# A gated decoder layer on one NeuronCore: another split of the contraction in the gate stage, and two vector operations placed later

## The chip, the cores and the metric

One core of a Trainium2 chip runs the whole layer in one launch. The time is device microseconds (us), the median of three runs. TensorE (PE) multiplies, VectorE (DVE) and ScalarE (ACT) work beside it, SyncE (SP) issues most transfers from HBM and GpSimd (POOL) issues the rest. PE's granted clock was 0.999 of full speed.

## The reference, cut to what matters

```python
mod = jax.nn.silu(c) @ w_ada[l] + b_ada[l]                  # (2048) @ (2048, 6 * 2048)
sh1, sc1, gt1, sh2, sc2, gt2 = split(mod, 6)
h = rmsnorm(x, g_pre_mix[l]) * (1.0 + sc1) + sh1            # x: 256 tokens x 2048
proj = h @ w_in[l]            # GLA q/k/v/gate, a rank-16 factor, MoBA q/k/v, gate_a, gate_b
y_a = o_gla @ w_gla_out;  y_b = o_moba @ w_moba_out
merged = sigmoid(gate_a) * y_a + sigmoid(gate_b) * y_b
x = x + gt1 * rmsnorm(merged @ w_o, g_post_mix)
h = rmsnorm(x, g_pre_ffn) * (1.0 + sc2) + sh2
x = x + gt2 * rmsnorm(conv_ffn(h), g_post_ffn)              # up, conv of width 3, GELU gate, down
```

All is float32. A product is made of three passes: operands are split into a rounded part `hi` and a remainder `lo`, and hi*hi, hi*lo and lo*hi are summed in PSUM.

## The kernel before, in words

The contraction over 2048 channels runs over 16 k-tiles of 128. The kernel's first 232 us are the gate stage: columns `gate_a` and `gate_b` of `w_in` (4096 columns, eight blocks of 512). The trouble there is that `h` needs `sh1` and `sc1` first, which are themselves a product with 33.5 MB of `w_ada`. So the stage is cut along the contraction into five chunks, listed in `CHUNK`, and `K0` holds where each begins. For a chunk of n k-tiles the 16 pieces of `w_ada` that give its shift and scale are read first, each 128 x 2 x 128n elements. The text calls them units. DVE adds a unit times a column of silu(c) to `acc0` (`head_unit`, L978 and L981), PE turns the sum, DVE reduces it to `mods` (`shift_and_scale`, L1009 to L1014), ACT and DVE scale x to `h` and split it (`h_part`, `h_scale`, `h_lo`). This is called the turn to a chunk. Then PE works the chunk's eight slots, one for each block of 512 columns: a slot of n k-tiles is 6n matmuls of 512 columns (4n with `hi` weights, then 2n with `lo`). ACT rounds each slot's weights `raw` to `hi` (L561), DVE subtracts to get `lo` (L971). Partial sums are copied out of PSUM and back in between chunks (L640, L647), and the last chunk's are added by DVE (`gate_out`, L1110). Two slots for values lie in chunks 1 and 2, and one for the rank-16 columns (`W_LOW`) ahead of chunk 4.

What sets the order. SP issues in the order written: 16 units of chunk 0, then slot w's weights and two units of the next chunk (three at slots 5 and 6, none at slot 7), and so on, all on one queue. There are four `raw` buffers, so slot w's weights wait until PE has finished slot w-4 (`used`), and eight buffers for units, so a unit waits until DVE has used the one eight before it. DVE's order is written out too: in `for w in range(W_HEAD)` it takes some units (two, and four at the fifth slot of a chunk), then `split_lo(w + 3)`. At the fifth slot of chunk 2 it takes all of the first four units of chunk 4 before the `lo` of slot 7 of chunk 2, and the turn to chunk 3 follows that `lo`.

The first slot has only one chunk's worth of data to wait for and is worked in two halves (`first_slot`, `first_mods`): k-tiles 0 and 1, then the rest.

The other 67.1 MB of `w_ada` are 96 modulation units of 128 x 1024 elements, issued by POOL and added by DVE into `acc_a` or `acc_b` (`ada_unit`, L1000). Tables say how many DVE takes after each step: `UNITS_3` for the last nine slots of the gate stage, `UNITS_E`, `UNITS_H` and `UNITS_L` for the four heads, `UNITS_M` for the 16 steps of the merge. After the gate stage the first head step waits for the gate sum of slot 6 of chunk 4 (`gate_add`). In the merge DVE multiplies each block of 512 columns by its gates and adds (`merged`, L1287 to L1290), and PE transposes the result one step later (`merged_T`, L1848). The first steps of the output projection wait for all 96 modulation units.

Of the kernel before, what the change touches and what calls it, by code (L numbers as in the profile page):

```python
# [12 lines left out]
P = 128  # L13
# [3 lines left out]
def layer_kernel(nc, x, c, w_ada, b_ada, g_pre_mix, w_in, w_alpha_up, b_alpha, g_gla_head, w_gla_out,  # L17
# [28 lines left out]
    UP_ITERS = FFN // 256  # L46
    CHUNK = (3, 3, 3, 3, 4)
    NQ = len(CHUNK)
# [83 lines left out]

    UNITS_3 = {W_LOW + j: n for j, n in enumerate((0, 1, 1, 1, 2, 2, 2, 2, 1))}
    UNITS_H = [2, 1, 1, 1, 1, 1, 1, 2, 2, 2, 2, 2]
    UNITS_E = [2, 1, 1, 1, 1, 1, 0, 2, 2, 2, 2, 1]
    UNITS_L = [2, 1, 1, 1, 1, 1, 1, 2, 2, 1, 1, 1]
    UNITS_M = [0, 2, 2, 1, 1, 2, 0, 2, 1, 2, 1, 2, 1, 1, 0, 1]
    assert sum(UNITS_3.values()) + EARLY * sum(UNITS_E) + (HEADS - 1 - EARLY) * sum(UNITS_H) + sum(UNITS_L) + sum(UNITS_M) == 6 * KT

# [20 lines left out]
    with ctx:  # L160
# [207 lines left out]
        def _(sp):  # L368
# [41 lines left out]
            for w in range(W_HEAD):  # L410
                if w >= 4:
                    sp.wait_ge(used, w - 3)
                if w == 0:
                    c0 = C_GA + 512 * GATE_CB[0][0]
                    sp.dma_start(grid(0, 512)[:, 0:2, :], win[:, 0:2, c0:c0 + 512]).then_inc(half_in, 16)
                    for j in range(2):
                        cs = slice(256 * j, 256 * (j + 1))
                        fill(0, grid(0, 512)[:, 2:CHUNK[0], cs], win[:, 2:CHUNK[0], c0 + 256 * j:c0 + 256 * (j + 1)])
                elif w == W_LOW:
                    load_grid(w, win, 0, KT, C_LOW, P)  # L420
                elif GATE_SLOTS[w][0] == VALUE:
# [128 lines left out]
        def _(act):  # L550
# [72 lines left out]
            for k in range(2, CHUNK[0]):  # L623
                ins = act.activation(h32[:, k, :], xT[:, k, TOK:], ACT.Identity, bias=mods[:, M_SH1, k:k + 1], scale=mods[:, M_SC1, k:k + 1])
            link(ins)
            act.activation(hT[:, 2:CHUNK[0], 0:TOK], h32[:, 2:CHUNK[0], :], ACT.Copy).then_inc(first_hi, 1)
            act.wait_ge(arr[0], fills(0))
            act.activation(hi[:, 0, 1024:slot_elements(0)], raw[:, 0, 1024:slot_elements(0)], ACT.Copy).then_inc(hi_done, 1)
            split_hi(1)
# [320 lines left out]
        def _(dve):  # L950
# [91 lines left out]
            for half, done in ((0, unit_half), (1, unit_done)):  # L1042
                part = slice(256, P * CHUNK[0]) if half else slice(0, 256)
                a = acc0[:, 0, :, part]
                unit = unit_view(KT - 1)[:, :, part]
                dve.scalar_tensor_tensor(a, unit, scol[:, KT - 1:KT], a, ALU.mult, ALU.add).then_inc(done, 1)
            dve.wait_ge(cols_read, 3)

            def first_mods(half, done):
                qs = slice(2, CHUNK[0]) if half else slice(0, 2)  # L1050
                dve.wait_ge(done, 1)
# [7 lines left out]
            dve.wait_ge(xt_read, 1)  # L1059
            for k in (0, 1):  # L1060
# [479 lines left out]
        def _(pe):  # L1540
# [469 lines left out]
```

## Time and profile before

| | us |
|---|---|
| median of 3 runs | 1452.08 (1452.02 to 1455.47) |
| profiled execution, its own time | 1453.58 |
| its span, first to last instruction | 1451.8 |
| PE busy | 1420.3 (98%) |
| DVE busy | 1090.1 (75%) |
| ACT busy | 757.6 (52%) |
| chain that ended last | PE 88%, DMA 5%, DVE 4%, ACT 2% |

The span is the time from the first to the last instruction, and what lies around it is 1.8 us. PE is busy nearly all the time, so the time can change only where PE is idle, or if PE's own work changes. A transfer's landing is read from the row of the first instruction that waited for it: its start, where the idle time before it was ended by that DMA. A row with xN stands for N instructions in a row.

### The profile page before, as it was taken

The numbers are of one execution on the slowest core, as the hardware profiler recorded it, in microseconds if no ns is written. First come the engines' busy times: TensorE is split into PE (matmuls) and PEld (weight loads), VectorE is DVE, ScalarE is ACT, GpSimd is POOL, SyncE is SP. The second block draws the span as 40 slices with busy tenths as digits, with TensorE's granted clock in tenths as the row PEclk, the third lists the DMA queues.
The fourth block names the chain that finished last, engine by engine and source line by source line (L and its number), as shares of the span: only waits on it lengthen the run. The fifth ranks groups of instructions, "written<-read, shape, count | busy, mean of one in ns | idle before, by whom it ended". The sixth has DMA issues, their size and how long they took to land.

```text
span 1451.8 us, 19848 instructions
## 1 busy us (share of the span) xinstructions
PE 1420.3 (98%) x7298; PEld 1210.2 (83%) x7298; DVE 1090.1 (75%) x1163; ACT 757.6 (52%) x869; POOL 84.2 (6%) x165
## 2 busy tenths in 40 slices
PE   4999999999999999999999999999999999999998
PEld 3788778888888888878888888888888888888886
DVE  5999879988989888844887777787777666544545
ACT  6566663555545466334855445454455455344343
POOL 2000001111111111000000000000000000000000
PEclk9999999999999999999999999999999999999999
DMA  9999979988988878857486767676766565655553
GB/s 352 380 374 380 364 244 347 289 294 293 327 272 285 274 269 283 283 177 286 147 272 234 244 219 243 203 241 222 240 223 200 175 195 184 201 193 185 200 193 125
DMA packets 240570, 367.08 MB, mean 253 GB/s; under 512 B 12015, under 2 KB 178673, under 8 KB 239746
## 3 DMA queue, kind: packets, MB, share of 16 engines
q1 hardware_dynamic: 220576, 294.69, 61.1%
q0 software_dynamic: 18848, 69.23, 13.2%
q10 hardware_dynamic: 1090, 2.40, 0.4%
q8 instruction: 36, 0.59, 0.2%
q14 instruction: 20, 0.16, 0.0%
HBM read 364.18 MB, written 2.10 MB: 252 GB/s over the span
## 4 chain that ended last, share of the span: by engine, by line
PE 88%; DMA 5%; DVE 4%; ACT 2%; issue 1%; SPq 0%; DVEq 0%; ACTq 0%
PE ps L1542 87%; DMA raw<-in_w_in 2%; DVE acc L981 1%; DMA adar<-in_w_ada 1%; DMA ada<-in_w_ada 1%; ACT hi L561 1%; DMA raw<-in_w_gla_out 1%; DMA raw<-in_w_moba_out 0%; DVE lo L971 0%; DVE acc_a L1000 0%; DVE yt L1362 0%; PE ps L1848 0%; DVE x L1365 0%; SPq L405 0%; PE ps L1827 0%
## 5 line engine op out<-in xcount | busy, mean ns | idle before, releaser
L1542 PE MATMUL ps<-hT,hi 128*128 128x512 f32 x1936 | 465.8, 393 | 1.7 <-DVE GA L1110 0.9
L1542 PEld LDWEIGHTS ps<-hT,hi 128*128 128x128 f32 x1936 | 356.1, 188 | 72.7 <-DVE GA L1110 1.3
L561 ACT ACTIVATE hi<-raw 128x2048 fp32r<-128x2048 f32 (+1 forms) x123 | 222.3, 1808 | 238.1 <-DMA raw<-in_w_in 154.2
L971 DVE TENSOR_TENSOR lo<-raw,hi 128x2048 fp32r<-128x2048 f32 (+1 forms) x123 | 264.7, 2153 | 77.1 <-ACT hi L561 76.7
L1542 PEld LDWEIGHTS ps<-hT,lo 128*128 128x128 f32 x1920 | 246.1, 191 | 9.8 <-DVE lo L971 0.5
L1542 PE MATMUL ps<-hT,lo 128*128 128x256 f32 x1920 | 249.2, 283 | 0.1
L1490 DVE TENSOR_TENSOR lo<-raw,hi 128x2048 fp32r<-128x2048 f32 x88 | 199.0, 2290 | 32.5 <-ACT hi L914 32.3
L1542 PE MATMUL ps<-hi,hT 128*128 128x512 f32 x768 | 186.7, 393 | 2.2 <-ACT hi L561 1.9
L1542 PE MATMUL ps<-hi,asp 128*128 128x512 f32 x704 | 175.9, 389 | 0.0
L1542 PEld LDWEIGHTS ps<-hi,hT 128*128 128x128 f32 x768 | 142.1, 188 | 35.0 <-issue 4.5
L914 ACT ACTIVATE hi<-raw 128x2048 fp32r<-128x2048 f32 x88 | 165.9, 1906 | 8.8 <-DMA raw<-in_w_up 7.5
L1542 PEld LDWEIGHTS ps<-hi,asp 128*128 128x128 f32 x704 | 132.1, 188 | 27.4
L1521 DVE TENSOR_TENSOR lo<-raw,hi 128x2048 fp32r<-128x2048 f32 x40 | 91.7, 2292 | 49.7 <-ACT hi L936 49.7
L546 POOL DMA_DIRECT2D ada<-in_w_ada x128 | 67.7, 530 | 676.2 <-DVE acc_a L1459 294.7
L1542 PE MATMUL ps<-lo,hT 128*128 128x512 f32 x384 | 96.6, 390 | 0.4 <-DVE lo L971 0.2
L1542 PE MATMUL ps<-lo,asp 128*128 128x512 f32 x352 | 96.1, 389 | 0.0
L892 ACT ACTIVATE cv<-ps 128x512 f32<-128x512 f32 x44 | 26.4, 600 | 133.6 <-PE ps L1542 133.6
L981 DVE SCALAR_TENSOR_TENSOR acc<-adar,scol,acc 128x768 f32<-128x768 f32 (+1 forms) x73 | 78.1, 1071 | 12.4 <-DMA adar<-in_w_ada 8.7
L1542 PEld LDWEIGHTS ps<-lo,hT 128*128 128x128 f32 x384 | 71.9, 188 | 16.1 <-DVE lo L971 0.7
L903 ACT ACTIVATE asp<-aT 128x256 fp32r (+1 forms) x44 | 18.0, 416 | 124.5 <-PE ps L1542 124.5
L896 ACT ACTIVATE cv<-up,cols 128x256 f32<-128x256 f32 x88 | 48.2, 595 | 56.7 <-DVE up L1472 56.7
L1542 PEld LDWEIGHTS ps<-lo,asp 128*128 128x128 f32 x352 | 66.0, 188 | 14.0 <-DVE lo L971 0.4
(265 smaller groups left out, 1312.2 us busy)
## 6 DMA issues: line engine op xcount, KB each, us to landing
raw<-in_w_up SPq DMA_DIRECT2D x176, 512.0 KB, 4.4
raw<-in_w_in SPq DMA_DIRECT2D x146, 512.0 KB, 6.1
ada<-in_w_ada POOLq DMA_DIRECT2D x128, 512.0 KB, 5.4
raw<-in_w_down SPq DMA_DIRECT2D x88, 512.0 KB, 4.2
adar<-in_w_ada SPq DMA_DIRECT2D x64, 384.0 KB, 8.9
raw<-in_w_o SPq DMA_DIRECT2D x32, 512.0 KB, 4.7
adar<-in_w_ada SPq DMA_DIRECT2D x16, 512.0 KB, 9.9
raw<-in_w_gla_out SPq DMA_DIRECT2D x16, 512.0 KB, 4.9
```

The lines of the kernel that those rows point to most:

```text
L546: pool.dma_start(unit_buffer(u), wada[:, t, PART_COL[part]:PART_COL[part] + 1024]).then_inc(ada_in[unit_slot(u)], 16)
L561: act.activation(hi[:, w % 4, 0:n], raw[:, w % 4, 0:n], ACT.Copy).then_inc(hi_done, 1)
L892: act.activation(cv[:, :, :], ps[:, 2 * g:2 * g + 2, TOK:], ACT.Copy).then_inc(cross5, 1)
L896: act.activation(cv[:, ct, :], up[:, ct, 2:], ACT.Identity, scale=cols[:, ds(f + COL_CONV + 4 * FT, 1)], bias=cols[:, ds(f + COL_CB, 1)]). ...
L903: act.activation(asp[:, k, 0:TOK], aT[:, ds(kt, 1), :], ACT.Copy).then_inc(a_hi, 1)
L914: act.activation(hi[:, w % 4, :], raw[:, w % 4, :], ACT.Copy).then_inc(hi_done, 1)
L971: dve.tensor_tensor(lo[:, w % 4, 0:n], raw[:, w % 4, 0:n], hi[:, w % 4, 0:n].bitcast(F32), ALU.subtract).then_inc(lo_done, 1)
L981: ins = dve.scalar_tensor_tensor(a, unit_view(u), scol[:, t:t + 1], a, ALU.mult, ALU.add)
L1490: dve.tensor_tensor(lo[:, k, :], raw[:, k, :], hi[:, k, :].bitcast(F32), ALU.subtract).then_inc(lo_done, 1)
L1521: dve.tensor_tensor(lo[:, k, :], raw[:, k, :], hi[:, k, :].bitcast(F32), ALU.subtract).then_inc(lo_done, 1)
L1542: return pe.matmul(out_, lhsT, rhs, start=start, stop=stop, skip_group_check=open_sum)
```

## The change

`CHUNK` becomes 2, 3, 3, 4, 4. The first slot has two k-tiles now and is worked as k-tile 0, then k-tile 1 (`FIRST = 1`). One modulation unit leaves the table of the gate stage (slot 5 of chunk 4), one leaves step 10 of the merge, and one each is added at steps 13 and 15. The number of matmuls, of units and of bytes stays as it was.

```diff
-    CHUNK = (3, 3, 3, 3, 4)
+    CHUNK = (2, 3, 3, 4, 4)
+    FIRST = 1
...
-    UNITS_3 = {W_LOW + j: n for j, n in enumerate((0, 1, 1, 1, 2, 2, 2, 2, 1))}
+    UNITS_3 = {W_LOW + j: n for j, n in enumerate((0, 1, 1, 1, 2, 2, 1, 2, 1))}
...
-    UNITS_M = [0, 2, 2, 1, 1, 2, 0, 2, 1, 2, 1, 2, 1, 1, 0, 1]
+    UNITS_M = [0, 2, 2, 1, 1, 2, 0, 2, 1, 2, 0, 2, 1, 2, 0, 2]
...
-                    sp.dma_start(grid(0, 512)[:, 0:2, :], win[:, 0:2, c0:c0 + 512]).then_inc(half_in, 16)
+                    sp.dma_start(grid(0, 512)[:, 0:FIRST, :], win[:, 0:FIRST, c0:c0 + 512]).then_inc(half_in, 16)
...
-            act.activation(hi[:, 0, 0:1024], raw[:, 0, 0:1024], ACT.Copy).then_inc(half_hi, 1)
+            act.activation(hi[:, 0, 0:512 * FIRST], raw[:, 0, 0:512 * FIRST], ACT.Copy).then_inc(half_hi, 1)
...
-                part = slice(256, P * CHUNK[0]) if half else slice(0, 256)
+                part = slice(P * FIRST, P * CHUNK[0]) if half else slice(0, P * FIRST)
...
-                    ks = range(2, CHUNK[0]) if half else range(2)
+                    ks = range(FIRST, CHUNK[0]) if half else range(FIRST)
```

On SP's queue at the start of the program, before (`adar` are units, `raw` weights; the last number of a unit is 128n):

```order
L405 DMA adar<-in_w_ada 128x2x384 x16
L415 DMA raw<-in_w_in 128x2x512
L370 DMA raw<-in_w_in 128x256 x2
L405 DMA adar<-in_w_ada 128x2x384 x2
L370 DMA raw<-in_w_in 128x512
L370 DMA raw<-in_w_in 128x2x512
```

and now:

```order
L406 DMA adar<-in_w_ada 128x2x256 x16
L416 DMA raw<-in_w_in 128x512
L371 DMA raw<-in_w_in 128x256 x2
L406 DMA adar<-in_w_ada 128x2x384 x2
L371 DMA raw<-in_w_in 128x512 x2
```

The first 16 units are a third smaller, and so are the first slots' weights, while the units between them, which are chunk 1's, keep their size.

On DVE around the turn to chunk 3, before (`acc_90` takes units; the reduce and the two rows behind it make the shift and scale):

```order
L971 TENSOR_TENSOR lo<-raw,hi 128x1536
L978 TENSOR_SCALAR acc_90<-adar,scol 128x1024
L981 SCALAR_TENSOR_TENSOR acc_90<-adar,scol,acc_90 128x1024 x3
L971 TENSOR_TENSOR lo<-raw,hi 128x1536
L1009 TENSOR_REDUCE mods<-ps 128x2x3
L1012 TENSOR_TENSOR mods<-mods,cols 128x2x3
L1014 SCALAR_TENSOR_TENSOR mods<-mods,cols 128x3
```

and now:

```order
L972 TENSOR_TENSOR lo<-raw,hi 128x1536
L979 TENSOR_SCALAR acc_90<-adar,scol 128x1024
L982 SCALAR_TENSOR_TENSOR acc_90<-adar,scol,acc_90 128x1024 x3
L972 TENSOR_TENSOR lo<-raw,hi 128x1536
L1010 TENSOR_REDUCE mods<-ps 128x2x4
L1013 TENSOR_TENSOR mods<-mods,cols 128x2x4
L1015 SCALAR_TENSOR_TENSOR mods<-mods,cols 128x4
```

The order is the same: four units of chunk 4, a `lo`, the reduce. The reduce covers four k-tiles now.

On DVE between the gate sums of slots 5 and 6 of chunk 4, before:

```order
L1110 TENSOR_TENSOR GA<-GA,ps 128x2x512
L971 TENSOR_TENSOR lo<-raw,hi 128x2048
L1000 SCALAR_TENSOR_TENSOR acc_a<-ada,scol,acc_a 128x1024
L1000 SCALAR_TENSOR_TENSOR acc_a<-ada_114,scol,acc_a 128x1024
L1110 TENSOR_TENSOR GA<-GA,ps 128x2x512
```

and now:

```order
L1111 TENSOR_TENSOR GA<-GA,ps 128x2x512
L972 TENSOR_TENSOR lo<-raw,hi 128x2048
L1001 SCALAR_TENSOR_TENSOR acc_a<-ada,scol,acc_a 128x1024
L1111 TENSOR_TENSOR GA<-GA,ps 128x2x512
L972 TENSOR_TENSOR lo<-raw,hi 128x2048
```

One unit of two is gone. In the merge the single unit ahead of `merged` for block 2 (L1287) is gone in the same way.

## Rows read from the trace of the kernel before

**Rows 1.** Busy time of each engine, clock, DMA share and GB/s, by stretch.
```profile
core 0: us, PE busy (x) PEld busy (x) DVE busy (x) ACT busy (x) POOL busy (x), PEclk, DMA share, GB/s
20.00:140.00 120.00, 116.56 (x525) 94.24 (x524) 107.89 (x107) 77.16 (x83) 0.00 (x0) 1.00 1.06 377
140.00:160.00 20.00, 20.00 (x93) 16.58 (x92) 19.42 (x18) 11.98 (x13) 0.00 (x0) 1.00 1.05 386
176.00:232.00 56.00, 55.42 (x249) 44.70 (x247) 43.91 (x39) 30.96 (x25) 6.98 (x14) 1.00 0.86 280
```
**Rows 2.** PE's waits over the span: total us, times, longest.
```profile
PE ps L1542 <- ACT hi L561: 1.9, 4, 0.9
PE ps L1848 <- DVE GA L1290: 1.0, 2, 0.7
```
**Rows 3.** PE's timeline: start, duration, [idle before it, ended by].
```profile
30.02 1.16 PE L1542 MATMUL ps<-hi,hT 128*128 128x512 f32 x4
35.18 3.06 PE L1542 MATMUL ps<-hi,hT 128*128 128x512 f32 x12 [0.38 <-ACT hi L561]
...
145.48 1.52 PE L1542 MATMUL ps<-hi,hT 128*128 128x512 f32 x6
...
171.02 2.99 PE L1542 MATMUL ps<-hi,hT 128*128 128x512 f32 x12 [0.38 <-ACT hi L561]
...
202.26 3.79 PE L1542 MATMUL ps<-hi,hT 128*128 128x512 f32 x16
...
207.70 3.79 PE L1542 MATMUL ps<-hi,hT 128*128 128x512 f32 x16
...
225.82 3.79 PE L1542 MATMUL ps<-hi,hT 128*128 128x512 f32 x16
```
**Rows 4.** PE's timeline, first step of the heads.
```profile
232.28 3.94 PE L1542 MATMUL ps<-hT,hi 128*128 128x512 f32 x16 [0.86 <-DVE GA L1110]
```
**Rows 5.** ACT's timeline, the last transposed x and the first weights.
```profile
26.12 0.43 ACT L596 ACTIVATE xT<-ps 128x256 f32<-128x256 f32 x1
28.00 1.06 ACT L616 ACTIVATE hi<-raw 128x1024 fp32r<-128x1024 f32 x1 [1.45 <-DMA raw<-in_w_in]
```
**Rows 6.** ACT's timeline, rounding of slots' weights as they land.
```profile
75.67 1.50 ACT L561 ACTIVATE hi<-raw 128x1536 fp32r<-128x1536 f32 x1 [0.63 <-DMA raw<-in_w_in]
...
80.79 1.92 ACT L561 ACTIVATE hi<-raw 128x2048 fp32r<-128x2048 f32 x1 [2.71 <-DMA raw<-in_w_in]
...
169.39 1.49 ACT L561 ACTIVATE hi<-raw 128x1536 fp32r<-128x1536 f32 x1 [1.28 <-DMA raw<-in_w_in]
```
**Rows 7.** DVE's timeline at the turn to chunk 3.
```profile
137.23 2.67 DVE L981 SCALAR_TENSOR_TENSOR acc<-adar,scol,acc 128x1024 f32<-128x1024 f32 x2 [0.75 <-DMA adar<-in_w_ada]
139.82 1.75 DVE L971 TENSOR_TENSOR lo<-raw,hi 128x1536 fp32r<-128x1536 f32 x1
141.56 0.96 DVE L1009 TENSOR_REDUCE mods<-ps 128x6 f32<-128x768 f32 x1
```
**Rows 8.** ACT's timeline at the same turn.
```profile
143.00 1.10 ACT L607 ACTIVATE h<-xT,mods 128x256 f32<-128x256 f32 x2 [0.90 <-DVE mods L1014]
144.13 0.63 ACT L611 ACTIVATE hT<-h 128x512 fp32r<-128x512 f32 x1
```
**Rows 9.** DVE's timeline ahead of the gate sum of slot 6.
```profile
228.42 2.67 DVE L1000 SCALAR_TENSOR_TENSOR acc_a<-ada,scol,acc_a 128x1024 f32<-128x1024 f32 x2
231.01 1.21 DVE L1110 TENSOR_TENSOR GA<-GA,ps 128x1024 f32<-128x1024 f32 x1
```
**Rows 10.** DVE's timeline in the merge, ahead of the transposes of block 2.
```profile
589.47 1.28 DVE L1000 SCALAR_TENSOR_TENSOR acc_b<-ada,scol,acc_b 128x1024 f32<-128x1024 f32 x1
```
**Rows 11.** PE's timeline, the transposes of block 2.
```profile
594.32 1.09 PE L1848 MATMUL ps<-ident,GA 128*128 128x128 f32 x8 [0.67 <-DVE GA L1290]
```
**Rows 12.** DVE's timeline at the end of the merge.
```profile
608.83 2.29 DVE L971 TENSOR_TENSOR lo<-raw,hi 128x2048 fp32r<-128x2048 f32 x1 [1.78 <-ACT hi L561]
...
621.00 0.69 DVE L1296 TENSOR_TENSOR mT<-ps,mT 128x512 fp32r<-128x512 f32 x1 [2.18 <-ACT mT L770]
```

More of the change, by code:

```diff
@@ L414, in _ @@
                     c0 = C_GA + 512 * GATE_CB[0][0]
-                    sp.dma_start(grid(0, 512)[:, 0:2, :], win[:, 0:2, c0:c0 + 512]).then_inc(half_in, 16)
+                    sp.dma_start(grid(0, 512)[:, 0:FIRST, :], win[:, 0:FIRST, c0:c0 + 512]).then_inc(half_in, 16)
                     for j in range(2):
                         cs = slice(256 * j, 256 * (j + 1))
-                        fill(0, grid(0, 512)[:, 2:CHUNK[0], cs], win[:, 2:CHUNK[0], c0 + 256 * j:c0 + 256 * (j + 1)])
+                        fill(0, grid(0, 512)[:, FIRST:CHUNK[0], cs], win[:, FIRST:CHUNK[0], c0 + 256 * j:c0 + 256 * (j + 1)])
                 elif w == W_LOW:
@@ L615, in _ @@
             act.wait_ge(half_in, 16)
-            act.activation(hi[:, 0, 0:1024], raw[:, 0, 0:1024], ACT.Copy).then_inc(half_hi, 1)
+            act.activation(hi[:, 0, 0:512 * FIRST], raw[:, 0, 0:512 * FIRST], ACT.Copy).then_inc(half_hi, 1)
             act.wait_ge(first_ready, 1)
             act.wait_ge(xt_read, 2)
-            for k in range(2):
+            for k in range(FIRST):
                 ins = act.activation(h32[:, k, :], xT[:, k, TOK:], ACT.Identity, bias=mods[:, M_SH1, k:k + 1], scale=mods[:, M_SC1, k:k + 1])
@@ L622, in _ @@
             act.wait_ge(mods_ready, 1)
-            for k in range(2, CHUNK[0]):
+            for k in range(FIRST, CHUNK[0]):
                 ins = act.activation(h32[:, k, :], xT[:, k, TOK:], ACT.Identity, bias=mods[:, M_SH1, k:k + 1], scale=mods[:, M_SC1, k:k + 1])
             link(ins)
-            act.activation(hT[:, 2:CHUNK[0], 0:TOK], h32[:, 2:CHUNK[0], :], ACT.Copy).then_inc(first_hi, 1)
+            act.activation(hT[:, FIRST:CHUNK[0], 0:TOK], h32[:, FIRST:CHUNK[0], :], ACT.Copy).then_inc(first_hi, 1)
             act.wait_ge(arr[0], fills(0))
-            act.activation(hi[:, 0, 1024:slot_elements(0)], raw[:, 0, 1024:slot_elements(0)], ACT.Copy).then_inc(hi_done, 1)
+            act.activation(hi[:, 0, 512 * FIRST:slot_elements(0)], raw[:, 0, 512 * FIRST:slot_elements(0)], ACT.Copy).then_inc(hi_done, 1)
             split_hi(1)
@@ L1049, in first_mods @@
             def first_mods(half, done):
-                qs = slice(2, CHUNK[0]) if half else slice(0, 2)
+                qs = slice(FIRST, CHUNK[0]) if half else slice(0, FIRST)
                 dve.wait_ge(done, 1)
@@ L1059, in _ @@
             dve.wait_ge(xt_read, 1)
-            for k in (0, 1):
+            for k in range(FIRST):
                 ins = dve.tensor_scalar(hT[:, k, 0:TOK], xT[:, k, TOK:], mods[:, M_SC1, k:k + 1], mods[:, M_SH1, k:k + 1], ALU.mult, ALU.add)
@@ L1064, in _ @@
             dve.wait_ge(half_hi, 1)
-            dve.tensor_tensor(lo[:, 0, 0:1024], raw[:, 0, 0:1024], hi[:, 0, 0:1024].bitcast(F32), ALU.subtract).then_inc(half_lo, 1)
+            dve.tensor_tensor(lo[:, 0, 0:512 * FIRST], raw[:, 0, 0:512 * FIRST], hi[:, 0, 0:512 * FIRST].bitcast(F32), ALU.subtract).then_inc(half_lo, 1)
             dve.wait_ge(first_h, 1)
             dve.wait_ge(first_h32, 1)
-            dve.tensor_tensor(hT[:, 0:2, TOK:], h32[:, 0:2, :], hT[:, 0:2, 0:TOK].bitcast(F32), ALU.subtract).then_inc(h_ready, 1)
+            dve.tensor_tensor(hT[:, 0:FIRST, TOK:], h32[:, 0:FIRST, :], hT[:, 0:FIRST, 0:TOK].bitcast(F32), ALU.subtract).then_inc(h_ready, 1)
             dve.wait_ge(first_hi, 1)
-            second = slice(2, CHUNK[0])
+            second = slice(FIRST, CHUNK[0])
             dve.tensor_tensor(hT[:, second, TOK:], h32[:, second, :], hT[:, second, 0:TOK].bitcast(F32), ALU.subtract).then_inc(h_ready, 1)
             dve.wait_ge(hi_done, 1)
-            rest = slice(1024, slot_elements(0))
+            rest = slice(512 * FIRST, slot_elements(0))
             dve.tensor_tensor(lo[:, 0, rest], raw[:, 0, rest], hi[:, 0, rest].bitcast(F32), ALU.subtract).then_inc(lo_done, 1)
@@ L1611, in unit_sums @@
             def unit_sums(half, values, vector, first):
-                js = range(2, CHUNK[0]) if half else range(2)
+                js = range(FIRST, CHUNK[0]) if half else range(FIRST)
                 for j in js:
```

## The prediction

> **What bounds the kernel now.** I read the page first: PE is busy 98% of the span and its clock is full, so the change can win only idle time of PE, 1451.8 - 1420.3 = 31.5 us in all. PE's first weight matmul starts at 30.02 [rows 3], and from 20 to 140 us PE is idle 3.4 [rows 1]. The table of PE's waits then names what is left: four waits for ACT's rounding and two for the merged gate products are 2.9 us together [rows 2], and one at the first head step is 0.86 us [rows 4]. The change goes for three of these places: the start, the head step, the merge.
>
> Next I asked what PE waits for in the gate stage. The table by stretch has the 16 DMA engines busy at 1.05 to 1.06 of their time, at 377 to 386 GB/s, from 20 to 160 us; only after 176 us do they fall to 0.86 [rows 1]. ACT's timeline shows the same from the other end: each slot's weights are rounded the moment they land, and that is so at the fourth slot of chunk 1 (75.67) and still at slot 6 of chunk 3 (169.39) [rows 6]. PE's timeline has its last wait of this kind at 171.02 [rows 3]: 169.39 landed, 1.49 rounded, 0.14 to the first matmul. So up to 171 us two streams run side by side, DMA and PE, nearly equal, and DMA touches PE at both ends. From 171.02 PE runs alone. An earlier start of PE is worth something only if what lands last for it lands earlier too.
>
> One k-tile of a slot costs PE (207.70 - 202.26)/4 = 1.36 us [rows 3]. Per k-tile of the contraction that is 8 x 1.36 = 10.9 us of matmuls, against 2.1 MB of units and 2.1 MB of weights, 11.1 us at 377 GB/s. Neither stream can get far ahead.
>
> **The change part by part.**
>
> The start. The first 16 units shrink from 6.29 to 4.19 MB. Before, the first weights landed at 28.00 and PE began at 30.02 [rows 3, 5]. Now 2.1 MB less stand ahead of the weights, 5.6 us, and the transposed x takes their place: ACT writes its last part until 26.55 [rows 5], then rounds 512 columns for about 0.6, estimated from the 1.06 that 1024 took, and PE begins at about 27.3. That is 2.7 us sooner. It is a head start, not yet a gain.
>
> Chunks 0 to 2. In chunk 0 PE's slots take 2.72 us, but each brings two k-tiles of weights and two three-wide units, 1.31 MB, 3.5 us at 377 GB/s. In chunk 2 the units between the slots are chunk 3's and four wide: 1.84 MB, 4.8 us, against PE's 4.08. PE waits again and again, several us in all. These waits eat the head start and are not summed, since a later landing decides.
>
> The turn to chunk 3. I count bytes ahead of the landing that matters. Ahead of the third and fourth units of chunk 4 the queue carries all 64 units of chunks 0 to 3, which are 12 k-tiles wide in both versions, the same two units of chunk 4, and 24 slots of weights plus one. Only those weights differ: 8 slots x 9 k-tiles before, 8 x 8 now, so 8 x 0.262 = 2.1 MB less, 5.4 us at 386 GB/s. The number of rows in the units is the same, 64 units of 256 rows. So the landing moves from 137.23 [rows 7] to 131.8. Behind it DVE's order is unchanged: two units 2.59, the `lo` 1.74, the reduce and what follows 1.44 until ACT's scale at 143.00, which is a third wider now, 0.3 more by the reduce's 0.96 for six columns against eight. Then ACT scales 1.13 and rounds 0.63 [rows 7, 8]. Sum: 131.8 + 2.59 + 1.74 + 1.44 + 0.3 + 1.13 + 0.63 = 139.6. Before, the same chain ended at 144.76 and PE came to it only at 145.48 [rows 3], so 0.72 was hidden; now PE is there first. PE begins chunk 3 at 139.7, 5.8 us earlier than before. But it has 64 k-tiles in front of it instead of 56, 8 x 1.36 = 10.9 us more. Before, from 171.02 with 38 k-tiles left, the stage ended at 225.82 + 5.44 = 231.26 [rows 3]: 51.7 of matmuls and 8.56 of other work (one set of transposes, the rank-16 slot, small products). Now it ends at 139.7 + 87.0 + 8.56 = 235.3. That is 4.0 us later.
>
> The lower bound of this term comes from the weights of slot 6 of chunk 3 alone: one k-tile less ahead of them (0.7 us), landing at 168.7, rounding 1.92 [rows 6] and 0.14, then 40 k-tiles, 54.4 and 8.56: 233.7, 2.5 us later. Slots 1 to 5 give the same within 0.2, since each step back adds 1.36 of work and takes 0.68 of bytes and PE's slack of before. The upper bound is 5.5: the turn with another landing 1.5 us late, twice DVE's own wait of 0.75 there [rows 7]. I take 4.0, because DVE's order leaves no way round the chain.
>
> The gate sum of slot 6. One unit fewer, 2.67/2 = 1.3 us, stands ahead of it [rows 9]. It ended at 232.22 and would end 1.3 earlier against PE's slots, ahead of the end of slot 7 (231.26 before). PE's first head step gains the whole gap, 232.28 - 231.26 = 1.0 [rows 3, 4]. If the cover is gone elsewhere it gains nothing: 0 to -1.0. I take -1.0.
>
> The merge. One unit less, 1.28 us (589.47), stands ahead of the products of block 2, more than the wait of 0.67 before their transposes, which goes [rows 10, 11]. -0.7, bounds -0.8 and 0. The two added units cost PE nothing by the rows. At step 13 DVE is idle 1.78 before the `lo` at 608.83, more than one unit's 1.33. At step 15 DVE is idle 2.18 before 621.00, more than that again [rows 12]. Their two transfers start one or two units later, with three buffers between, and need to be there 5 us after. If that cover failed, each would cost up to 1.3.
>
> Sum: +4.0 - 1.0 - 0.7 = +2.3 us. On the profiled execution, 1453.58, that is 1455.9; its time lies 1.5 above the median of the runs. On the median: 1452.08 + 2.3 = 1454.4.
>
> **The rivals.** 0.3%, 4.4 us, is about what a measurement can tell from no change: faster is below 1447.7, slower above 1456.4.
>
> *PE's head start is kept.* The queue is then not what feeds PE late in the gate stage, and the 2.7 us, the 1.9 us of waits for ACT, the 1.0 and the 0.7 all come off: 1445.8. For it: the start is the largest gap there is, and from 140 to 160 PE has no idle time at all [rows 1]. Against it: DMA share of 1.05 throughout [rows 1], and the landing at 169.39 [rows 6]. The Trainium skill (Perfetto Trace Analysis, Optimization Strategies) would side with it: keep the matmul engine as busy as possible and work on what blocks it. By that rule the head start counts; by rows 1 it is given back. 7%.
>
> *The turn is not late.* DVE's chain hides behind the weights, and only the landings hold: +2.5 - 1.7, 1452.9. For it: DVE was idle 0.75 at that point. Against it: the chain is written in that order, and it had only 0.72 to spare, with PE then 5.8 us later than now. 20%.
>
> *The units' places don't matter.* The waits at the first head step and at the merge stay, because DVE is held there by transfers of modulation units: 1452.08 + 4.0 = 1456.1. 9%.
>
> *Slower: the queue runs dry in the first 25 us.* Eight units in flight are 2.1 MB now, not 3.1, 5.6 us of transfer, and DVE must free each buffer. Every us in which DMA idles or slows there reaches the landing at 131.8 and so the end, one for one. It decides from 2.1 us on. With 3 us lost: 1457.4. For it: rows of 1 KB move slower. The value slot between the landings at 75.67 and 80.79 carries 1.05 MB in such rows and 0.79 MB of units: 5.12 us less 2.1 leaves 3.0, about 348 GB/s [rows 6]. For 4.19 MB that is only 12.0 us against 11.1, and it is balanced by the wider rows of chunk 3's units. Against it: by an estimate from 1.28 us for 1024 columns [rows 10], DVE needs 0.7 to 0.8 us a unit, and DMA 0.75 at 348 GB/s, so neither leaves the other far behind. The Trainium skill (Perfetto Trace Analysis, DMA Optimizations) says that transfers under 2 KB carry a significant overhead. If it is meant per row, the trace agrees, a tenth at 1 KB; the sum by 348 instead of 377 for those 4.19 MB alone would be 0.9 us more. 14%.
>
> **How the numbers follow.** The forecast has 50%, the rivals 7, 20, 9 and 14. Faster is the first rival, 7%, and slower the last, 14%. The rest, 79%, is within 0.3%. The forecast's own range is 1452.9 to 1455.9, by its lower bound and the upper one. The whole range reaches to 1449.3 below, midway between the first two rivals, and to 1457.4 above, the last one.
>
> **What would show it.** In the profile of the changed kernel: the first weight matmul near 27.3; chunk 3's first slot on PE near 139.7, with the wait before it on ACT's `hT` or DVE's `lo`; no wait of PE for weights in slots 1 to 6 of chunk 3; the end of slot 7 of chunk 4 at about 235; no wait for L1111 ahead of the heads, and one instead of two for L1291. DMA share stays over 1.04 from 20 to 160 us. It would be wrong if PE began chunk 3 before 138, or if the gate stage ended before 232, or if DMA fell below 370 GB/s between 10 and 60 us.

## The result, and the profile after

The changed kernel is slower. Its median is 1459.5 us of 7 runs (1458.2 to 1461.2), against 1452.1 of 7 of the kernel before: ratio 1.0046 [1.0036, 1.0056]. The forecast was 1454.4, at most 1457.4. The profiled execution took 1458.15 (span 1456.4), 4.6 more than the one before. So the profiles show 4.6 us, and 2.1 (by the ratio) to 2.8 (by the medians) more are in the other runs.

First the same stretches as in [rows 1], then the first 26 us of both kernels, before above, after below.

```profile
20.00:140.00 120.00, 112.53 (x496) 90.01 (x496) 107.74 (x110) 74.69 (x84) 0.00 (x0) 1.00 1.05 377
140.00:160.00 20.00, 18.39 (x81) 15.29 (x82) 19.50 (x16) 12.18 (x12) 0.00 (x0) 1.00 1.06 387
176.00:232.00 56.00, 56.00 (x256) 45.56 (x255) 41.54 (x36) 30.38 (x25) 5.93 (x12) 1.00 0.82 262
```
```profile
0.00:26.00 26.00, 7.73 (x44) 7.10 (x44) 14.03 (x16) 16.21 (x30) 10.74 (x28) 1.00 0.97 341
18.00:20.00 2.00, 1.60 (x8) 1.57 (x8) 1.79 (x3) 2.00 (x3) 0.00 (x0) 1.00 1.06 373
22.00:24.00 2.00, 2.00 (x12) 2.00 (x11) 1.90 (x2) 1.67 (x6) 0.00 (x0) 1.00 1.06 373
```
```profile
0.00:26.00 26.00, 8.30 (x39) 7.67 (x40) 11.44 (x18) 16.27 (x29) 10.07 (x28) 1.00 0.95 308
18.00:20.00 2.00, 1.80 (x8) 1.39 (x8) 1.79 (x3) 2.00 (x2) 0.00 (x0) 1.00 1.03 334
20.00:22.00 2.00, 1.24 (x6) 1.24 (x7) 1.79 (x3) 1.88 (x6) 0.00 (x0) 1.00 0.96 286
22.00:24.00 2.00, 2.00 (x11) 2.00 (x10) 1.69 (x4) 1.61 (x6) 0.00 (x0) 1.00 0.91 221
```

From 30 to 160 us DMA is as full as before. But in the first 26 us it moved 33 GB/s less: 0.86 MB, 2.3 us of transfer at 377 GB/s. Some of that is the rows of 1 KB, which move at 347 GB/s with every DMA engine busy (14 to 18 us); the rest is a hole in the queue's work from 19 to 25 us. PE is idle 8% from 140 to 160, where it was never idle, and not at all from 176 to 232.

PE's waits after 25 us, cut to those that the text uses, to be held against [rows 2]:

```profile
PE ps L1543 <- DVE lo L972: 3.0, 5, 1.3
PE ps L1543 <- ACT hT L612: 2.5, 2, 1.8
PE ps L1652 <- DVE acc L982: 2.0, 1, 2.0
...
PE ps L1543 <- ACT hi L562: 0.7, 1, 0.7
PE ps L1849 <- DVE GA L1291: 0.7, 1, 0.7
PE ps L1781 <- ACT ot L688: 0.4, 1, 0.4
```

The timeline of PE: first weight matmul, unit sums of chunk 1, last slot of chunk 2, chunk 3, first head step, transposes of blocks 0 and 2 of the merge. They answer to [rows 3, 4, 11].

```profile
29.52 0.82 PE L1543 MATMUL ps<-hi,hT 128*128 128x512 f32 x2
...
55.06 0.88 PE L1652 MATMUL ps<-ident,acc 128*128 128x128 f32 x6 [1.97 <-DVE acc L982]
...
138.16 1.67 PE L1543 MATMUL ps<-lo,hT 128*128 128x512 f32 x6 [0.87 <-DVE lo L972]
141.61 2.06 PE L1543 MATMUL ps<-hi,hT 128*128 128x512 f32 x8 [1.78 <-ACT hT L612]
...
237.20 3.79 PE L1543 MATMUL ps<-hT,hi 128*128 128x512 f32 x16
...
564.74 1.09 PE L1849 MATMUL ps<-ident,GA 128*128 128x128 f32 x8 [0.65 <-DVE GA L1291]
599.24 1.04 PE L1849 MATMUL ps<-ident,GA 128*128 128x128 f32 x8
```

And DVE and ACT behind it, for [rows 5 to 9]: DVE in the start and at the turn to chunk 3, then ACT's first weights and its part of the turn. The reciprocal needs a square root from ACT (`stat`), which comes at 15.9 us in both kernels. Before, DVE was busy with units up to that point and did not wait; this is its row:

```profile
16.08 0.15 DVE L1036 RECIPROCAL stat<-stat 128x2 f32<-128x2 f32 x1
```

And after:

```profile
15.93 0.17 DVE L1037 RECIPROCAL stat<-stat 128x2 f32<-128x2 f32 x1 [1.46 <-ACT stat L582]
16.13 7.60 DVE L982 SCALAR_TENSOR_TENSOR acc<-adar,scol,acc 128x512 f32<-128x512 f32 x9
...
133.76 2.67 DVE L982 SCALAR_TENSOR_TENSOR acc<-adar,scol,acc 128x1024 f32<-128x1024 f32 x2 [0.74 <-DMA adar<-in_w_ada]
138.02 1.22 DVE L1010 TENSOR_REDUCE mods<-ps 128x8 f32<-128x1024 f32 x1
...
234.40 1.22 DVE L1111 TENSOR_TENSOR GA<-GA,ps 128x1024 f32<-128x1024 f32 x1
```
```profile
26.72 0.63 ACT L617 ACTIVATE hi<-raw 128x512 fp32r<-128x512 f32 x1
...
137.78 1.92 ACT L562 ACTIVATE hi<-raw 128x2048 fp32r<-128x2048 f32 x1 [3.88 <-DMA raw<-in_w_in]
139.72 1.09 ACT L608 ACTIVATE h<-xT,mods 128x256 f32<-128x256 f32 x2
```

The end of the gate stage went from 231.26 to 237.20 and waits for nothing there. The start of the heads moved by 237.20 - 232.28 = 4.9 us, the end of the span by 4.6. After the merge nothing differs. In ACT's rows, its part of the turn (L608) starts when ACT's own rounding of the weights of chunk 3's first slot ends, 139.70, and DVE's modulation is ready at 139.63: two chains end together there.

### The profile page after: what moved, and what is told of

The parts are those of the page before. It is cut to its first block, busy times and chain, and to the rows that moved or that the text cites. A ratio compares the mean times of both kernels' runs of the same rounds, so it can differ in the third digit from the quotient of the medians.

```text
span 1456.4 us, 19836 instructions
## 1 busy us (share of the span) xinstructions
PE 1421.1 (98%) x7292; PEld 1210.8 (83%) x7292; DVE 1089.3 (75%) x1163; ACT 756.2 (52%) x868; POOL 83.6 (6%) x165
## 4 chain that ended last, share of the span: by engine, by line
PE 90%; DVE 3%; DMA 3%; ACT 2%; issue 1%; POOL 1%; SPq 0%; DVEq 0%; POOLq 0%; ACTq 0%
PE ps L1543 89%; DMA raw<-in_w_in 2%; DVE acc L982 1%; ACT hi L562 1%; DMA raw<-in_w_moba_out 1%; PE ps L1626 0%; DVE yt L1363 0%; ACT xn L591 0%; ACT junk L580 0%; DVE x L1366 0%; DVE lo L972 0%; PE ps L1849 0%; PE ps L1828 0%; ACT h32b L830 0%; POOL maskf L506 0%
## 5 line engine op out<-in xcount | busy, mean ns | idle before, releaser
L562 ACT ACTIVATE hi<-raw 128x2048 fp32r<-128x2048 f32 (+2 forms) x123 | 222.7, 1812 | 239.1 <-DMA raw<-in_w_in 153.4
L972 DVE TENSOR_TENSOR lo<-raw,hi 128x2048 fp32r<-128x2048 f32 (+2 forms) x123 | 265.3, 2157 | 82.0 <-ACT hi L562 82.0
L982 DVE SCALAR_TENSOR_TENSOR acc<-adar,scol,acc 128x768 f32<-128x768 f32 (+2 forms) x73 | 78.7, 1078 | 12.1 <-DMA adar<-in_w_ada 8.1
```

Of the source, the lines that this page charges most:

```text
L562: act.activation(hi[:, w % 4, 0:n], raw[:, w % 4, 0:n], ACT.Copy).then_inc(hi_done, 1)
L972: dve.tensor_tensor(lo[:, w % 4, 0:n], raw[:, w % 4, 0:n], hi[:, w % 4, 0:n].bitcast(F32), ALU.subtract).then_inc(lo_done, 1)
L982: ins = dve.scalar_tensor_tensor(a, unit_view(u), scol[:, t:t + 1], a, ALU.mult, ALU.add)
```

## The experiments

Ratios are to the kernel before, from runs on the same chip. A ratio's interval is about 0.001 to each side, 1.5 us, so single steps are read from pairs and from traces.

**e1: only the tables.**
```diff
-    UNITS_3 ... (0, 1, 1, 1, 2, 2, 2, 2, 1)
+    UNITS_3 ... (0, 1, 1, 1, 2, 2, 1, 2, 1)
-    UNITS_M = [0, 2, 2, 1, 1, 2, 0, 2, 1, 2, 1, 2, 1, 1, 0, 1]
+    UNITS_M = [0, 2, 2, 1, 1, 2, 0, 2, 1, 2, 0, 2, 1, 2, 0, 2]
```


> The kernel before with the two tables of the units alone (one unit less in slot 6 of chunk 4 of the gate stage; merge units 2 at the end instead of 1). The chunks and the first slot are as before. My theory: the first heads no longer wait 1.09 us for the gate sum of slot 6 (-1.0); in the merge the wait of 0.84 us before block 2 goes, but two waits that the changed kernel showed (0.42 us at 460, 0.34 us more at 565) come in its place, so the merge gives 0 to -0.3. Sum -1.0 to -1.3 us: 1450.8 to 1451.1 us, ratio about 0.9992. The prediction had -1.7 for these two. Rival (the places of single units don't matter at the end): 1452.1, ratio 1.000. Slower than 1453 speaks against both.


Measured: 1451.3 us of 12 runs, 0.9984 [0.9974, 0.9994], a gain of 2.3 us, or 1.3 by the medians. The wait at the first head step and the one before block 2 are gone, and the wait for GA at block 0 grew from 0.31 to 1.25. In the kernel before, the two places together are worth what I expected, and the loss is elsewhere.

**e9: the gate's table alone** (the merge's unit stays at step 10; step 15 takes one more).


> The kernel before with one unit less in slot 6 of chunk 4 and one more at the end of the merge; the unit before block 2 of the merge stays where it was. It splits e1 (ratio 0.9984): by the two traces the gate's wait of 0.9 to 1.1 us goes and the merge's wait of 0.7 to 0.8 stays. Theory: ratio 0.999, 1451.3 us, that is the gate's share is 1.0 and the merge's 0.3 or less. 8 of 20 runs of the kernel before lay over 1454 us and none of 12 of e1: if the wait at 232 us sets them off they are gone here too; if it is the one at 594, they stay. Rival: it was the place before block 2 that gave e1 its gain, then the ratio here is 1.000.


Measured: 1.0004 [0.9995, 1.0013], 1452.4 us. The gain of 1.0 is not seen in the time, though the head step waits no more. Its profiled execution (span 1455.7) shows one way in which runs can differ: PE waits 2.6 us for GA at block 0, and then its clock is half from 562 to 566. Two of its 11 runs are over 1457, while none of the 15 runs of the kernel before beside them is over 1453.4. Not settled: which half of e1 brings its gain.

**e2: only chunks and first slot** (the changed kernel with the old tables).


> The changed kernel with the old tables of the units: chunks 2, 3, 3, 4, 4 and the single k-tiles of the first slot alone. If the parts add up, this is the changed kernel plus what the tables gave there (1.0 to 1.3 us): ratio to the kernel before 1.0053 to 1.0060, some 1460 us, with the wait of the first head for the gate sum of slot 6 back at about 1 us. If the tables gave nothing the ratio is that of the changed kernel, 1.0046. If it were the tables that made the kernel slower (units at the end of the merge), it is below 1.003.


Measured: 1.0044 [1.0029, 1.0059]. The whole loss is the chunks'. Its profile (span 1455.0) also answers a point that I had wrong: the wait at the first head step did not come back with the old table. The gate sum of slot 6 ends before PE needs it, DVE above, PE below:
```profile
235.24 1.21 DVE L1111 TENSOR_TENSOR GA<-GA,ps 128x1024 f32<-128x1024 f32 x1
```
```profile
236.51 3.93 PE L1543 MATMUL ps<-hT,hi 128*128 128x512 f32 x16
```
So with the new chunks the gate's table has no wait left to remove, and e2 and the changed kernel are the same by their ratios. Why DVE is in time here is open.

**e13: only the first slot by single k-tiles** (chunks 3, 3, 3, 3, 4, `FIRST = 1`).


> The kernel before (chunks of 3, 3, 3, 3 and 4, old tables), with the first slot worked by single k-tiles: one k-tile first, then two, instead of two and one. This is the part of the head start alone. My theory, that DMA sets the turn to chunk 3, gives 0 (1452.1 us, ratio 1.000), PE starts its first weight matmul up to 1 us sooner and begins chunk 3 at 145.5 as before. Rival (the start is on the path to the end): 0.5 to 1 us less, 0.9995. A second rival, that splitting the first slot differently costs by itself: more than 1.001.


Measured: 1.0006 [0.9996, 1.0017]. The finer first slot neither gains nor costs what can be told. It gave no head start either: in its profile the first weight matmul comes at 31.17, 1.15 later than before, and the clock is half for some 4 us from 30 on. Yet chunk 3 begins at 145.48 as before, so PE's later start cost nothing at the turn.

**e3: sixteen buffers for the first sixteen units**, which are half as wide as a buffer and fit in pairs. SP issues them (the expectation says ACT).
```diff
+            if u < KT:
+                return adar[:, u % 8, 512 * (u // 8):512 * (u // 8 + 1)]...
             return adar[:, u % 8, 0:2 * P * n]...
```


> The changed kernel, but the first sixteen modulation units (half as large as the later ones) have sixteen buffers instead of eight, so ACT issues them without waiting for DVE; nothing else moves. Theory 'the queue runs dry': the DMA engines no longer fall to 221 to 286 GB/s between 20 and 24 us, the third and fourth unit of chunk 4 land at about 131.8 us instead of 133.76, PE begins chunk 3 near 139.7 instead of 141.61, and the end moves 1.9 us forward: about 1457.5 us by the median of the changed kernel, ratio 1.0033. Rival (what the queue loses early is not on the path; PE's work bounds from the start on): no change, ratio 1.0046, with PE's start of chunk 3 at 141.6.


The trace: the hole is closed, and the third unit of chunk 4 lands where the prediction had it.
```profile
20.00:22.00 2.00, 1.33 (x6) 1.33 (x7) 1.72 (x3) 1.88 (x6) 0.00 (x0) 1.00 1.09 360
22.00:24.00 2.00, 2.00 (x12) 2.00 (x12) 1.76 (x3) 1.61 (x6) 0.00 (x0) 1.00 1.07 365
```
```profile
131.99 1.28 DVE L990 SCALAR_TENSOR_TENSOR acc<-adar,scol,acc 128x1024 f32<-128x1024 f32 x1 [0.75 <-DMA adar<-in_w_ada]
```
```profile
139.99 2.06 PE L1551 MATMUL ps<-hi,hT 128*128 128x512 f32 x8 [1.81 <-ACT hT L620]
```
PE begins chunk 3 at 139.99 (forecast 139.7), the heads at 235.58 (235.3), and the span is 1453.2, 3.2 under the changed kernel's. But the median of its 7 runs is 1459.5, 1.0047 [1.0030, 1.0063], from 1454.9 to 1464.1: by the time there is no gain.

One profile against one says little of the size, since the landing also moves from execution to execution. All profiles with chunks 2, 3, 3, 4, 4 and DVE's order as in the changed kernel up to the turn give this:

| | third unit of chunk 4 lands, us |
|---|---|
| eight buffers | 133.76 (the changed kernel), 133.00 (e2), 132.76 (e10), 132.74 (e7), 132.68 (e17), 132.34 (after_again) |
| sixteen buffers | 132.21 (e14), 132.04 (e12), 131.99 (e3), 131.94 (e8) |

No profile with sixteen is later than one with eight, and the means are 132.88 and 132.05. So the buffers are worth 0.8 us on average, and the first profile of the changed kernel is the extreme of its kind, with the deepest hole (221 GB/s at 22 to 24 us; 254 to 360 in the other five).

**e4: the turn ahead of two units** (DVE takes two of the four units before the turn to chunk 3 behind it).


> The changed kernel, but DVE takes two of the four units of chunk 4 that stand between the units of chunk 3 and the turn after the turn instead of ahead of it. Theory A (DVE's chain from the landing of those units over lo, reduction, modulation, h ends the wait of PE): chunk 3 begins on PE 1.4 to 1.8 us sooner, ratio 1.0035. Theory B (ACT's order: it rounds slot (3,0) of the weights, which lands late by its place in the queue, ahead of its part of h, so DVE's earlier modulation finds ACT busy): no change at the end, ratio 1.0046, and DVE is through with the modulation 1 to 2 us earlier without PE starting earlier. I hold B the likelier, 60 to 40.


Measured: 1.0042 [1.0026, 1.0057], no gain. ACT's timeline:
```profile
136.52 1.91 ACT L562 ACTIVATE hi<-raw 128x2048 fp32r<-128x2048 f32 x1 [3.90 <-DMA raw<-in_w_in]
138.34 1.08 ACT L608 ACTIVATE h<-xT,mods 128x256 f32<-128x256 f32 x2
```
DVE had the modulation ready at 135.9 and ACT took it up at 138.34, when the weights of slot (3, 0) had come and were rounded. Theory B holds: the two chains that end together in the changed kernel both hang on the queue, and a shorter one on DVE gains nothing. The same trace shows three stretches of PE at half clock, each behind a wait (1.98, 2.88 and 2.97 us):
```profile
54.00:58.00 4.00, 4.00 (x15) 3.33 (x16) 3.90 (x6) 2.41 (x4) 0.00 (x0) 0.64 1.06 379
140.00:144.00 4.00, 3.78 (x10) 2.98 (x11) 4.00 (x5) 2.51 (x3) 0.00 (x0) 0.57 1.05 386
566.00:570.00 4.00, 3.54 (x14) 3.06 (x15) 3.90 (x4) 4.00 (x5) 0.00 (x0) 0.64 0.85 322
```

**after_again: the changed kernel once more.**


> The changed kernel once more, unchanged, beside the next three. Its first profile had a span of 1456.4 us with the clock of TensorE at half only behind the last matmuls, while the median of its runs was 2.8 us further from the kernel before than the two profiles were. Theory 'clock': in most executions a wait of PE of some 2 us in the gate stage (before the unit sums at 53 to 55, or the turn at 138 to 141.6) is followed by some 4 us at half clock, 2 us each; a second profile shows at least one such stretch in two cases of three, and its span is then 1457.5 to 1460. Rival 'DMA': the spread comes from the time at which transfers land, and the clock stays 1.00 to the end. Median about 1459, ratio 1.0046.


Measured: 1.0042 [1.0029, 1.0056]. Its profile has the clock at half behind the turn, as my theory had it, where the first profile had 1.00:
```profile
140.20 2.98 PE L1543 MATMUL ps<-hi,hT 128*128 128x512 f32 x8 [1.79 <-ACT hT L612]
142.97 2.72 PE L1543 MATMUL ps<-lo,hT 128*128 128x512 f32 x8
```
The same 16 matmuls took 5.3 us instead of 3.7. Chunk 3 began 1.4 us sooner than in the first profile, and the heads began later (237.42). But the span is 1454.9, not the 1457.5 to 1460 that I expected, and 1.5 below the first profile's: there is no wait in the merge. So the clock, the landing (132.34 against 133.76) and the merge all differ between executions of one kernel.

**e7: PE kept busy in two waits.**
```diff
             def next_sums(q):
+                if q == 1:
+                    keep_busy(7)
...
+                if (q, s) == (3, 0):
+                    pe.wait_ge(sum_read, 3)
+                    keep_busy(6)
```


> The changed kernel with 7 matmuls of no use in the wait before the unit sums of chunk 1 (53.1 to 55.1 us) and 6 in the wait for h at the turn to chunk 3 (139.8 to 141.6): 0.25 us each, so both fit into the waits (1.7 and 1.5 us). Their results are not read. Theory 'clock': the profiled span stays at 1456.4 (or loses 0.2), but the median falls to it plus 1.7 us, 1457.5 to 1458.3, ratio 1.0035, and the runs spread less. Rival: the median stays at 1459.3, ratio 1.0046, with the same spread.


Measured: span 1453.9 with the clock at 1.00, but 1.0057 [1.0043, 1.0071]. Against my theory, by the time. The trace bears out one part: the wait of 1.97 before the sums is filled but for 0.34.

**e8: sixteen buffers and kept busy.**


> The changed kernel with sixteen buffers for the first sixteen units (in the run e3 its profiled span was 1453.2, 3.2 us under the changed kernel, PE's start of chunk 3 139.99 instead of 141.61, but its median unchanged) and the 13 matmuls of no use in the two waits. If both losses are real and independent (1.9 us of DMA time in the first 25 us, and the clock behind the waits), the median is 1454.5 to 1456, ratio 1.0020, about what was predicted for the changed kernel. If the queue's loss is not on the path, it is that of e7. If the clock theory is wrong, it is that of e3, 1.0047.


Measured: 1.0044 [1.0030, 1.0058]. Two of its five runs are at 1455.0 and 1455.6, three at 1459.3 to 1459.7, and nothing lies between. A jump of 4 us is about the size of one long wait for GA in the merge and its clock (e4's wait is 3.0 us, its clock 1.6 by an estimate from after_again). No profile of these runs shows it.

**e10: the units of the merge spread** (steps 0 to 4: 1, 2, 1, 1, 0 instead of 0, 2, 2, 1, 1; step 12: 2 instead of 1).


> The changed kernel with two modulation units less ahead of the first block sum of the merge (steps 2 and 4 of the merge one unit less, steps 0 and 12 one more). In the ten executions profiled so far PE's wait for GA at the transposes of block 0 (559 to 566 us) was 0, 0.3, 0.7, 1.3, 2.6 or 3.0 us, and the two long ones were followed by 4 us at half clock (1.6 us more); the long ones are those in which two units stood back to back on DVE just before, so that their buffers were refilled beside the load of slot moba_out, which landed 10 us after its issue instead of 6.4. Theory 'merge wait': most unprofiled executions of the changed kernel have the long wait, and this is why its median lies 2.8 us over its profile; then this kernel's runs lose their upper group (over 1458) and the median is 1455 to 1456.5, ratio 1.0025, with the wait at 0. Rival: the upper group has another cause, median 1459, ratio 1.0045.


Measured: 1458.4, 1.0035 [1.0022, 1.0047], and all six runs lie between 1456.8 and 1458.8. Nothing is above 1459 any more, where five of the changed kernel's seven were; but four of the six are still over 1458, the median is 1.9 us above the range that I expected, and the interval overlaps that of the changed kernel. The theory is borne out in part at most.

**e12: e10 with sixteen buffers.**


> The changed kernel with sixteen buffers for the first sixteen units and the spread of e10. By the two theories together (1.9 to 3 us from the queue that no longer runs dry, and no long merge wait) 1452.5 to 1454.5 us, ratio 1.0010, and the runs close together. If only the queue theory is right: as e3, 1.0045. If only the merge theory: as e10.


Measured: 1457.1, 1.0027 [1.0017, 1.0038], eight runs within 1.7 us. The buffers gain 1.2 us here, by the ratios, against 1.9 to 3 expected.

**e17: e10 with PE kept busy. e14: all three.**


> The changed kernel with the units of the merge spread as in e10 and the 13 matmuls, its buffers as they are. Its partner is e10 (1458.4 us, ratio 1.0035). Theory 'clock': 1456.5 to 1457.2, ratio 1.0025. Rival: 1458.4. The difference to e14 is again the queue's: e14 should be 1.0 to 1.9 us faster.

> The changed kernel with sixteen buffers for the first sixteen units, the units of the merge spread as in e10, and the 13 matmuls of no use in PE's waits at 53 to 55 and 140 to 142 us. Its partner is e12 (the same without these matmuls: 1457.1 us, ratio 1.0027, all eight runs within 1.7 us). Theory 'clock': in most executions a stretch of 4 us at half clock follows the wait at the turn, and costs 1.6 to 2 us; the matmuls avoid it: 1455.2 to 1456.0 us, ratio 1.0018. Rival (the clock behind that wait isn't what the runs lose): 1457, ratio 1.0027.


Measured: e17 1457.2, 1.0030 [1.0020, 1.0041]; e14 1456.5, 1.0023 [1.0014, 1.0032]. Keeping PE busy gains 0.6 (e12 to e14) and 0.7 us (e10 to e17) by the ratios, about half of what I expected; the buffers gain 1.0 (e17 to e14). Each step is below its interval. Without the spread the same steps scatter: keeping PE busy is 2.2 us slower from after_again to e7 and 0.4 faster from e3 to e8, and the buffers are 1.9 faster from e7 to e8. What the traces show is firmer. Nine profiles have the first chunk of two and none of these matmuls, so they wait 2.0 us at 52 to 55 us, and in six of them the clock fell behind that wait. In the four profiles with the matmuls (e7, e8, e14, e17) it stayed full from there to the last 15 us of the span.

**e6: the reciprocal behind seven units instead of five.**


> The changed kernel with one line of DVE's moved: the reciprocal for the norm of x stands behind the first seven units, not behind the first five. In the changed kernel DVE waits for it 1.46 us (till 15.93) with landed units standing in its eight buffers, and DMA falls to 334, 286 and 221 GB/s between 18 and 24 us. One look, for the cause of that gap and not for the time. Theory: the gap comes from DVE being held there; then DVE has no wait or a short one at 15.9, the units end at most 1 us earlier (23.7 before) and DMA keeps above 330 GB/s until 22 us. Rival: the units, 0.84 us each on DVE against 0.76 us of transfer at 347 GB/s, are too slow by themselves: then the gap stays about as long.


One run, 1457.6 us (1451.6 for the kernel before beside it), taken for its trace. The hole is gone: 349, 354 and 376 GB/s from 18 to 24 us, and DVE is through at 23.1 instead of 24.7. So it came from DVE being held, and not from the units' own pace alone. But the third unit of chunk 4 landed no sooner:
```profile
133.80 2.68 DVE L982 SCALAR_TENSOR_TENSOR acc<-adar,scol,acc 128x1024 f32<-128x1024 f32 x2 [0.75 <-DMA adar<-in_w_ada]
```
ACT's timeline has the slots 1.8 us ahead of the changed kernel's until 78.73, and level with them at 103.00. PE had been at half clock at 54 to 59, and DMA moved 372 GB/s from 85 to 95, where the changed kernel has 387. e3 had the same clock stretch and kept its lead. Where e6 lost it is open, and with it whether a closed hole is enough by itself to bring the landing forward.

**e16: chunks 2, 3, 4, 3, 4.**


> The changed kernel with chunks of 2, 3, 4, 3, 4 instead of 2, 3, 3, 4, 4: the start is that of the changed kernel (small first units, the queue dry at 20 to 25 us), but the turn to chunk 3 has 9 k-tiles behind it as in the kernel before, and 7 ahead. My theory: the turn to chunk 3 lies where the kernel before has it (PE at 145.5) plus the 1 to 2 us that the queue lost, and the gate stage ends at 232 to 233.5 instead of 237.2: ratio 1.0005 to 1.0015, some 1453.5 us. Rival 'small first chunk': if what costs is the chunk of two at the start and the waits it brings at 53 to 60, the ratio stays above 1.003. Rival 'start is off the path': 0.9990, the tables' gain alone.


Measured: 1459.7, 1.0046 [1.0030, 1.0062]. My theory was wrong here. PE's last long wait for the queue is now the turn to chunk 2, with 11 k-tiles ahead:
```profile
101.56 3.31 PE L1543 MATMUL ps<-hi,hT 128*128 128x512 f32 x8 [2.05 <-ACT hT L612]
```
From there PE runs without such a wait, and the heads begin at 237.57, as in the changed kernel. A chunk of four at the third place puts the 16 wide units ahead of that turn. So by this trace it is not the place of chunk 3 that counts, but any turn whose units are late with much work still ahead. The rival on the small first chunk can't be excluded by this run.

**e11: e1 with the spread of e10.**


> The kernel before with the two tables of the change and the same spread of the units in the merge as in e10. e1 (ratio 0.9984) still waited 1.25 us for GA at 558.8 in its profile. Theory 'merge wait': this wait goes, 1449.5 to 1450.3 us, ratio 0.9975. Rival: the unit moved to step 12 or to step 0 makes another wait and it is 0.9984 again or worse.


Measured: 1451.2 of 12 runs, 0.9989 [0.9981, 0.9998]. The wait for GA at block 0 went, one of 0.7 for `oo` in the last head and one of 0.5 before block 2 came. No better than e1. Of all kernels run, e1 is the fastest by its ratio, 0.16% under the kernel before.

## Why the prediction was wrong, step by step

*What bounds the kernel.* Right: DMA at 377 to 387 GB/s up to 160 us, PE alone afterwards, no wait for weights in slots 1 to 6 of chunk 3, and the order of events at the turn: PE waited 1.78 there for ACT's `hT`.

*The start.* First weight matmul forecast 27.3, measured 29.52. ACT had the first weights rounded at 27.35, but PE's own order held it: transposes and the sums of unit 12 until 27.1, the sums of chunk 0 at 27.96, DVE's modulation at 28.57. It cost nothing, since a head start was "not yet a gain": in e13 PE began 1.15 later than before and was level at the turn.

*The step that failed* is the weighing of the first 25 us, "so neither leaves the other far behind", by which the landing at 131.8 and the turn at 139.7 were taken without loss. The estimate of 0.7 to 0.8 us for a unit on DVE was low: nine in a row took 7.60 us, 0.84 each, against 0.75 on the queue, so DVE can't make up a delay. And a delay was left out: with smaller units DVE was done with its first five before ACT's square root came, waited 1.46 us for it (15.93), landed units filled its eight buffers, and the queue ran dry. The prediction's own sign of being wrong, DMA under 370 GB/s between 10 and 60 us, is there: 334, 286 and 221 from 18 to 24. In this profile the landing came at 133.76, PE's chunk 3 at 141.61, the heads at 237.20: each 1.9 us late. Over the six profiles with eight buffers the landing is 0.5 to 2.0 us behind the forecast 131.8, with sixteen 0.1 to 0.4. In e3 the three are 131.99, 139.99 and 235.58, so the sum of bytes and the chain were right and this term was missing: 1.9 us in the first profile, more than the 1.5 that its upper bound allowed, 1.1 on average, 0.8 of it taken back by the buffers. It is the slower rival, at 14%: it reckoned one for one, decisive from 2.1 us lost, and 2.3 were lost in this profile, of which 1.9 reached the end. "Every us" is not always so: e6 won the time back at the start and lost it again.

*The gate sum of slot 6*, -1.0: the wait is gone as forecast (the sum begins at 234.40, PE comes at 237.20 without a wait), but this was not the moved unit's doing: e2 keeps the old table and has no wait either. So the number came by luck. In the kernel before, where the unit does remove the wait, the time of e9 doesn't show it.

*The merge*, -0.7: the wait before block 2 went (599.24), but block 0 waits 0.65 instead of 0.31 and a wait of 0.42 for `ot` came. From the start of the heads (+4.9) to the end (+4.6) only 0.3 was gained. By the ratios the old tables (e2, 1.0044) are no slower than the new ones (1.0046) with these chunks, so no part of the forecast -1.7 is seen as a gain of the tables.

*The profiled pair* is then 4.0 + 1.9 - 1.0 - 0.3 = 4.6, as measured.

*From the profile to the median.* I took the distance of the profile to the median (1.5) from the kernel before and gave it to the changed one. That step failed too, by 2.1 to 2.8 us. "These waits eat the head start and are not summed" counts a wait at its length. In nine of the eighteen executions profiled, PE's clock fell to half for about 4 us, once or more (the last 15 us of the span left aside): at 30 us, after the start, or behind a wait at 54, 102, 140 or 562 to 568 us. Behind the turn that cost 1.6 us by the 16 matmuls of after_again. By the ratios e17 and e14 show 0.6 to 0.7 us of it, and e10 1.0 (against after_again) to 1.6 (against the first runs), which I put down to the long wait in the merge. Taken in the order e10, e17, e14, the ratio of 1.0046 divides into 0.0023 that no experiment took away (3.3 us; forecast 2.3), 0.0007 with the buffers, 0.0005 with PE kept busy, 0.0011 with the merge spread. This is bookkeeping and not shown: each part is smaller than its interval, and e3, e7 and e8, without the spread, take nothing away. So what makes up the 2.1 to 2.8 us stays open in the main; the traces show only that the landing varies by 1.4 us, the clock takes 0 or 1.6 at the turn, and the wait at block 0 of the merge is 0 to 3.0. Whether the changed chunks bring the long wait in the merge more often than the old ones is not shown either. In three profiles it was 2.6 to 3.0 us (e4, e9, e16); in these DVE took two units back to back just before, and the load of `w_moba_out` needed 9.9 to 10.2 us from its issue to ACT's first use, in all others 5.5 to 9.0. But e7 and e1 had the same pair, with 6.7 us and no wait, and 8.5 us and a wait of 1.25.

*Rivals.* Head start kept: refuted. PE began 0.5 us sooner than before, and the heads began 4.9 later. The Trainium skill (Perfetto Trace Analysis, Optimization Strategies) has the matmul engine kept busy; here what counted was the queue behind it. Turn not late: refuted, PE waited 1.78 there. Units' places don't matter: refuted for the kernel before by e1 and its trace. In the changed kernel the waits are gone too, but e2 shows no loss with the old places.

## What to carry to other kernels

When a stage is made finer at its start, its transfers in flight shrink with it: hold each wait of the engine that frees the buffers against the bytes in flight, at the place where it stands, and not its mean pace. Cutting a contraction unevenly moves the point from which the matmul engine is alone, and the work left behind that point is what counts. Before a few us of a profiled execution are carried over to a median, look at how the runs spread, and take a second profile: here the same landing moved by 1.4 us between two profiles of one kernel, and a wait of 1.8 us cost 3.4 where the clock fell behind it.

## What the runs showed of the hardware

HBM to SBUF with all 16 engines busy: 347 GB/s in rows of 1 KB (14 to 18 us after), 373 in rows of 1.5 KB (16 to 24 us before), 387 where the units' rows are 2 KB (140 to 160 us after). The Trainium skill (Perfetto Trace Analysis, DMA Optimizations) says that transfers under 2 KB carry a significant overhead. Read per row, these numbers agree: a tenth is lost at 1 KB. The granted clock of PE fell from 2.4 to 1.2 GHz for some 4 us behind waits of 1.8 to 3.0 us (at 54, at a turn, in the merge) in some executions and not in others, even of the same kernel: behind 1.79 us at 140.20 in after_again it did, behind 1.78 at 141.61 in the first profile it did not. It fell at neither place in the four profiles in which PE worked through most of its waits at 52 to 55 us and at the turn.
